# A prompt attention stage with other leads, another order of its first loads, and its weighted sums with the low product first on 64 stationary columns

## The reference, cut to what matters

```python
def stick_breaking_block(q, k, v, q_pos, k_pos):
    z = jnp.einsum('bqhd,bkhd->bhqk', q, k).astype(jnp.float32) * (SB_HEAD_DIM ** -0.5)
    causal = k_pos[None, :] < q_pos[:, None]
    log_beta = jax.nn.log_sigmoid(z)
    log_rem = jnp.where(causal, log_beta - z, 0.0)
    tail = lax.cumsum(log_rem, axis=3, reverse=True) - log_rem
    w = jnp.where(causal, jnp.exp(log_beta + tail), 0.0)
    return jnp.einsum('bhqk,bkhd->bqhd', w.astype(v.dtype), v)

def mla_block(q_nope, q_rope, k_nope, k_rope, v, q_pos, k_pos):
    s = (jnp.einsum('bqhn,bkhn->bhqk', q_nope, k_nope)
         + jnp.einsum('bqhr,bkr->bhqk', q_rope, k_rope)).astype(jnp.float32)
    s = s * ((MLA_NOPE_DIM + MLA_ROPE_DIM) ** -0.5)
    visible = (k_pos[None, :] // CHUNK) <= (q_pos[:, None] // CHUNK)
    s = jnp.where(visible, s, jnp.finfo(jnp.float32).min)
    p = jax.nn.softmax(s, axis=-1)
    return jnp.einsum('bhqk,bkhv->bqhv', p.astype(v.dtype), v)
```

## Time and profile before

| | us |
|---|---|
| median of 3 runs | 2643.04 |
| lowest and highest | 2634.92, 2646.65 |
| the profiled execution, its own time | 2648.48 |
| span of its instructions | 2646.7 |
| prompt attention, first score matmul to last mix | 1089.1 to 2083.7 |
| a head in that stage (first transpose to the next head's first) | 122.9 |

### The profile page before, as it was taken

The page is one execution under the profiler, slowest core; times in us unless marked ns, Lnnn a source line. Parts: engine busy times, 40 slices in busy tenths (PEclk is TensorE's granted clock), DMA queues, the critical chain, the costliest instruction groups (busy, mean ns, idle before and its releaser), DMA issues. The chain is left out here.

```text
span 2646.7 us, 40141 instructions
## 1 busy us (share of the span) xinstructions
PE 2248.5 (85%) x12099; PEld 1869.0 (71%) x12099; DVE 1381.5 (52%) x2759; ACT 1323.5 (50%) x2852; POOL 776.9 (29%) x773
## 2 busy tenths in 40 slices
PE   6599996999977899498989999999989577775887
PEld 1488885899967677286868677777778356664765
DVE  2223232210137333487878778787878388863332
ACT  1223222211112433388888888888888555542221
POOL 0000000000000000356474737465563345542321
PEclk9799998899989899699999999999999777777989
DMA  8333322222337898733323343332320444426773
GB/s 292 106 101 95 108 83 89 100 80 82 116 92 198 284 310 290 158 67 69 68 66 75 70 91 67 68 82 58 74 54 23 107 136 135 142 67 196 177 185 93
DMA packets 304695, 314.44 MB, mean 119 GB/s; under 512 B 88322, under 2 KB 234765, under 8 KB 299489
## 3 DMA queue, kind: packets, MB, share of 16 engines
q1 hardware_dynamic: 299810, 297.45, 40.9%
q10 hardware_dynamic: 3744, 12.19, 1.2%
q0 software_dynamic: 992, 3.21, 0.3%
HBM read 194.83 MB, written 109.57 MB: 115 GB/s over the span
## 5 line engine op out<-in xcount | busy, mean ns | idle before, releaser
L1243 ACT ACTIVATE pa_whi<-banks 128x512 fp32r<-128x512 f32 (+3 forms) x640 | 346.4, 542 | 98.9 <-PE banks L1468 77.9
L1468 PE MATMUL banks<-ident,pa_p 128*128 128x128 f32 x2176 | 354.9, 279 | 2.2 <-ACT pa_p L1208 2.2
L1451 PE MATMUL banks<-pa_khi,pa_qst 128*128 128x512 f32 (+3 forms) x640 | 262.7, 410 | 103.9 <-DVE pa_p L1307 77.1
L1397 POOL TENSOR_TENSOR pa_wlo<-pa_whole,pa_whi 128x512 fp32r<-128x512 f32 (+2 forms) x240 | 279.2, 1172 | 191.4 <-ACT pa_whole L1248 190.7
L1379 POOL CAST pa_khi<-pa_kraw 128x512 fp32r<-128x512 f32 x64 | 39.1, 611 | 993.4 <-DMA pa_kraw<-scratch_sb_kT 993.4
L1468 PEld LDWEIGHTS banks<-ident,pa_p 128*128 128x128 f32 x2176 | 268.5, 143 | 61.4 <-issue 5.6
L1428 PE MATMUL banks<-pa_whi,pa_vst 128*128 128x512 f32 (+3 forms) x640 | 285.1, 445 | 1.5 <-POOL pa_wlo L1397 1.4
L1307 DVE TENSOR_TENSOR_SCAN pa_p<-banks,pa_p,pa_zero 128x512 f32<-128x512 f32 x192 | 246.3, 1283 | 71.4 <-ACT banks L1201 62.6
L1451 PEld LDWEIGHTS banks<-pa_khi,pa_qst 128*128 128x128 f32 x640 | 125.7, 196 | 184.2 <-DVE pa_p L1307 142.7
L1284 DVE TENSOR_TENSOR pa_wlo<-banks,pa_whi 128x512 fp32r<-128x512 f32 (+3 forms) x400 | 234.7, 587 | 27.0 <-ACT pa_whi L1243 27.0
L1452 PE MATMUL banks<-pa_klo,pa_qst 128*128 128x512 f32 (+3 forms) x640 | 242.6, 379 | 0.0
(11 more groups left out here) (231 smaller groups left out, 5095.6 us busy)
## 6 DMA issues: line engine op xcount, KB each, us to landing
ada<-in_ada_w_dram SPq DMA_DIRECT2D x6, 2048.0 KB, 11.4
scratch_sb_kT<-ke_kT SPq DMA_DIRECT2D x12, 1024.0 KB, 8.9
scratch_mla_kT<-ke_nT SPq DMA_DIRECT2D x12, 1024.0 KB, 5.5
scratch_mla_v<-ke_v SPq DMA_DIRECT2D x12, 1024.0 KB, 5.4
co_hlo<-scratch_hT SPq DMA_DIRECT2D x6, 1408.0 KB, 6.9
scratch_gatesT<-co_gates SPq DMA_DIRECT2D x12, 704.0 KB, 10.7
pr_x<-in_x_prompt_dram SPq DMA_DIRECT2D x16, 512.0 KB, 4.4
scratch_hT<-pr_hT SPq DMA_DIRECT2D x16, 512.0 KB, 5.3
```

The costliest lines, as they stand in the source:

```text
L1243: act.activation(whi[:, t % NW, q0:], bank, ACT.Copy).then_inc(hi_done, 1)
L1397: pool.tensor_tensor(wlo[:, t % NW, q0:], whole[:, t % 4, q0:], raw(whi[:, t % NW, q0:]), ALU.subtract).then_inc(pool_lo, 1)
L1451: pe.matmul(bank, qst[job][:, q], khi[job][:, keys], start=True, stop=False)
L1468: y = pe.transpose(ps[:, NS + t % NTB, x * P:(x + 1) * P], probs[g][x][:, i * P:(i + 1) * P], s["ident"][:])
```

## The change

Four edits, all in this stage.

- **Leads.** `LEAD` becomes two numbers: stick chunks run 18 ahead of the steps, softmax chunks 20. `chunks_at` says which chunks a step carries: steps 0 to 19 carry chunk t + 18; steps 20 and 21 carry two each (38 and 39; 40 and 41); steps 22 to 59 carry t + 20; steps 60 and 61 none; steps 62 to 79 carry chunk t - 62 of the next head. The last exponentials stay in steps 60 and 61. Head 0 starts with 18 chunks.
- **First loads.** k and q of the stick half come first, then the mask, `own_tile` and the rotary key, then v.
- **Waits.** TensorE waits at the first chunk of each group for the part of k that the group needs, and for the constants at the first softmax chunk only.
- **The products of a block.** `mix` takes the low product first and then the high one, except in the first block of a softmax group. The low product has only the high part of v as its stationary operand, 64 columns in place of 128, and writes 64 partitions of the bank. The product of the two low parts, which had been added in, is left out.

```diff
@@ constants
-    LEAD = 20
+    STICK_LEAD, SOFT_LEAD = 18, 20
...
@@ which chunks a step carries
-        def chunk_at(h, t, last):
-
-            if t + LEAD < HEAD:
-                return h, t + LEAD
-            return (None, 0) if last else (h + 1, t + LEAD - HEAD)
+        def chunks_at(h, t, last):
+
+            grown = JOB - SOFT_LEAD
+            if t < grown:
+                yield h, t + STICK_LEAD
+            elif t < grown + 2:
+                yield h, 2 * t - grown + STICK_LEAD
+                yield h, 2 * t - grown + STICK_LEAD + 1
+            elif t + SOFT_LEAD < HEAD:
+                yield h, t + SOFT_LEAD
+            if t + STICK_LEAD >= HEAD and not last:
+                yield h + 1, t + STICK_LEAD - HEAD
...
@@ SyncE, first loads
-                for job in range(2):
-                    load_k(0, job)
-                    load_q(0, job)
-                    load_v(0, job)
+                load_k(0, 0)
+                load_q(0, 0)
+                sp.dma_start(causal[:], d["const_causal"]).then_inc(const_loaded, 16)
+                sp.dma_start(probs[3][2][:, 0:CH], d["const_own_tile"]).then_inc(kr_loaded, 16)
+                for i in range(3):
+                    sp.dma_start(early[i * ROPE:(i + 1) * ROPE, 0:T], d["mla_krT"][:, 0:T]).then_inc(kr_loaded, 16)
+                load_v(0, 0)
+                load_k(0, 1)
+                load_q(0, 1)
+                load_v(0, 1)
...
@@ ScalarE, a step
-                    if last and t + LEAD in (HEAD, HEAD + 1):
-                        for g, i, c in exps_at(t + LEAD):
-                            exp(h, g, i, c)
-                    chunk(*chunk_at(h, t, last))
-
-                for m in range(LEAD):
+                    for which in chunks_at(h, t, last):
+                        chunk(*which)
+                    for g, i, c in exps_at(t + SOFT_LEAD):
+                        exp(h, g, i, c)
+
+                for m in range(STICK_LEAD):
...
@@ TensorE, mix
-                    for k, w in enumerate((whi, wlo)):
-                        mm = pe.matmul(ps[:, 6 + n % 2, q0:], vst[job][:, j, :], w[:, t % NW, q0:],
-                                       start=(job == 1 and j == 0 and k == 0), stop=(j == 4 * g + 3 and k == 1))
+
+                    first, done = job == 1 and j == 0, j == 4 * g + 3
+                    high = (ps[:, 6 + n % 2, q0:], vst[job][:, j, :], whi[:, t % NW, q0:])
+                    low = (ps[0:HD, 6 + n % 2, q0:], vst[job][:, j, 0:HD], wlo[:, t % NW, q0:])
+                    if first:
+                        pe.matmul(*high, start=True, stop=False)
+                        mm = pe.matmul(*low, start=False, stop=done)
+                    else:
+                        pe.matmul(*low, start=False, stop=False)
+                        mm = pe.matmul(*high, start=False, stop=done)
                     mm.then_inc(mixed, 1)
...
@@ TensorE, a chunk
+                    if (i, c) == (0, 0):
+
+                        wait_apart(pe, kv_split, kv_upto(h, "k", job) - PARTS + g + 1, passed)
                     if m % JOB == 0:
-                        wait_apart(pe, kv_split, kv_upto(h, "k", job), passed)
                         pe.wait_ge(q_loaded[job], (80 if job else 32) * (h + 1))
+                        if job:
+                            pe.wait_ge(const_done, 1)
```

More of the change, by code:

```diff
@@ L1036, in on_pool @@
         def on_pool(t):
-            return (t + LEAD) % HEAD < JOB and t % 4 != 3
+            return (t + SOFT_LEAD) % HEAD < JOB and t % 4 != 3
         POOLS = sum(on_pool(t) for t in range(HEAD))
@@ L1097, in _ @@
             def _(sp):
-                sp.dma_start(causal[:], d["const_causal"]).then_inc(const_loaded, 16)
-                for i in range(3):
-                    sp.dma_start(early[i * ROPE:(i + 1) * ROPE, 0:T], d["mla_krT"][:, 0:T]).then_inc(kr_loaded, 16)
-                sp.dma_start(probs[3][2][:, 0:CH], d["const_own_tile"]).then_inc(kr_loaded, 16)
                 def load_k(h, job):
@@ L1219, in chunk @@
                 def chunk(h, m):
-                    if h is None:
-                        return
-                    if m < 2 and not (isinstance(h, int) and h == 0):
-                        for g, i, c in exps_at(HEAD + m):
-                            exp(h - 1, g, i, c)
-                        if m == 0:
-                            return
-                        sigmoid(h, 0)
                     if m < JOB:
                         sigmoid(h, m)
-                    for g, i, c in exps_at(m):
-                        exp(h, g, i, c)
                 def finish(h, n):
@@ L1412, in _ @@
                 pe.sem_inc(mixed, NW)
-                pe.wait_ge(const_done, 1)
                 def mix(h, t):
```

2 lines of the change are left out of this document (removed).

## The result

The changed kernel takes 2653.47 us (median of 7 runs, 2650.74 to 2664.82), the kernel before 2644.38 (7 runs beside them, 2634.92 to 2647.82). The ratio over all runs is 1.0047, 95% interval 1.003 to 1.0065: slower by 9 us between the medians, where 17 us less were forecast. The time lies outside the range given, on the other side of no change.

The account below looks back on a forecast made before the run. TensorE was taken to bound softmax chunks (steps 20 to 59), three nearly equal engines the stick chunks. Terms -14.4 - 4 + 0 + 0 + 1.1 = -17.3 us gave 2631.2 from 2648.5, as a median 2626; range 2608 to 2646.

Parts of the forecast that it names:

- The low product on 64 columns: In mix behind the transposes: a shorter weight load saves 0.05 us a step, 14.4 us in softmax steps, 4 in stick.
- The comparison with the keys stage: Keys stage products with 64 stationary columns start 0.27 us apart, against 0.31 in mix; taken as evidence for 0.05 us saved.
- rival 2: In mix, the shorter weight load saves nothing, hidden or otherwise; the total becomes +1.1, 2644 us; chance 0.12.
- The leads: Across each head: 3.0 us gained at the boundary, 3.0 lost at steps 20 and 21; booked 0.
- Steps 20 and 21: Two chunks each: TensorE waits 0.75, 0.4 and 0.9 us; step 22 comes 5.8 us after step 20, 3.0 us lost.
- The boundary to step 68: Between heads, one wait of 4.55 us becomes two of 2.0 and 1.6; step 68 starts 2.6 us earlier.
- The 32 pairs from step 68 to 20: Step-and-chunk pairs after the boundary: as before, except two smaller chunks, about 0.4 us less.
- The loads: At the stage's start, the first scan waits for the rotary key and comes 1.1 us later.
- Rival 1: At the head boundary: waits at steps 20 and 21 shrink, up to 21 us more saved, about 2605 to 2612; chance 0.15.
- Rival 3: At steps 20 and 21 the clock drops and the boundary yields only 1.1 us: +9.6, 2653 us; chance 0.13.

Follow-up runs that it names:

- e1_products: Kernel before with only the products changed (low product first, on 64 columns): 2644.6 us, ratio 1.0013.
- e4_turned: Kernel before with the low product on 64 columns but behind the high one, except in a group's last block: 2648.4 us, ratio 1.0019.
- e5_both64: Kernel before with both products on 64 columns, high one first, some blocks excepted, part of the output left out: 2643.25 us in one run.
- e11_mix_last64: Kernel before with the output products moved behind the step's score products, low one first and on 64 columns: 2665.53 us, ratio 1.0074.
- e2_leads: Kernel before with the two leads alone (18 for stick chunks, 20 for softmax chunks): 2657.9 us, ratio 1.0063.
- e3_loads: Kernel before with the new order of first loads and the finer TensorE waits alone: 2645.96 us, ratio 1.0017.
- e6_half: Kernel before with three of a block's four transposes cut to 64 rows, part of the values left out: 2735.94 us in one run.
- e8_turn22: Kernel before with only the back edge of the loop over heads moved from step 12 to step 22: 2665.75 us, ratio 1.0064.

## Why the prediction was wrong

**The low product on 64 columns: forecast -14.4 and -4, measured 0. This step failed.** It read 0.07 to 0.08 us of a distance of 0.31 as waiting for weights. e1_products shows no gain, e4_turned and e5_both64 none with the load in question at 64 columns. What stands in the 0.31 us is worked out from the rows: the printed start of a matmul behind the transposes is no measure of when it begins to stream. Before, the weight loads behind the transposes of the earlier trace rows stand so:

```profile
1571.11 0.19 PEld L1428 LDWEIGHTS banks<-pa_whi,pa_vst 128*128 128x128 f32 x1
1571.22 0.19 PEld L1428 LDWEIGHTS banks<-pa_wlo,pa_vst 128*128 128x128 f32 x1
1571.46 0.19 PEld L1451 LDWEIGHTS banks<-pa_khi,pa_qst 128*128 128x128 f32 x1
```

In these rows a load runs one matmul ahead. The one at 1571.22 can start when the last transpose is through, and 0.24 us later, at 1571.46, the next one does, since the first product is through: 512 columns take no less anywhere in these rows. That leaves no wait for weights, and its printed start, 1571.14, is by my estimate about 0.08 us too early. After, the loads stand at 1570.98 and 1571.09, 0.11 apart although the first is 0.05 shorter. The comparison with the keys stage failed on what stands ahead, which the prediction called equally short: there it is matmuls of 64 columns, shorter than a load, as behind the mask's product in e11_mix_last64 (0.26); here it is transposes of 128 columns, whose starts are 0.11 us apart like those of the loads. This is rival 2, given 0.12. By the rule of the Trainium skill ("TensorE: Matmul & The Clock Gate", on the phases of a matmul), the next weights load under the present matmul; the trace agrees at the very place where I set it aside, and the mask's product (0.32 us with the wide load, 0.26 with the narrow one) shows its limit.

**The leads: forecast 0, measured +10.9 over six heads of the change and +6.8 in e2_leads, which has them alone (in the change with +4.2 in the last head, which has only the loss, and -2.2 in head 0). This step failed too.** The products and the loads add -0.7 and +1.0 by themselves. The other 4 us I put down to the clock (not tried apart): within the six heads it is at half for 44.4 us in the change and 34.1 in e2_leads. Before has 41.0, so the clock explains little of the change's loss and none of that of e2_leads. The parts of the 10.9:
- *Steps 20 and 21*: forecast 3.0 lost, measured 3.0 to 3.1. Right, wait by wait (0.66, 0.24 and 0.75 us for 0.75, 0.4 and 0.9).
- *The boundary to step 68*: forecast 2.6 gained, with one stretch of half clock. From step 60 to 68 it is 15.97 us before; after, 13.52 in heads with 3.4 us at half clock (2.45 gained) and 14.0 to 14.6 in heads with 6.8 (1.4 to 2.0 gained). In e2_leads a head with none takes 12.74. The walk was right for its clock. That the clock stays down for 6.8 us in most heads is no proof against the two short waits, though: e3_loads, which has the one wait of 4.55 us, has 6.8 us at all six boundaries, e5_both64 at five, e1_products at none. One of those of e3_loads:

```profile
1574.39:1581.21 6.82, 4.45 (x14) 3.67 (x15) 2.83 (x4) 4.38 (x12) 2.74 (x4) 0.50 0.91 204
```

- *The 32 pairs from step 68 to 20*: forecast 0.4 gained "as before". This failed. Before, and then two heads after:

```profile
1588.38:1638.06 49.68, 45.30 (x242) 33.86 (x241) 39.76 (x45) 42.65 (x92) 40.26 (x40) 0.97 0.18 41
```

```profile
1713.51:1764.41 50.90, 44.89 (x242) 33.81 (x241) 39.23 (x45) 42.73 (x93) 40.69 (x40) 0.97 0.19 44
1589.89:1639.66 49.77, 43.62 (x243) 32.65 (x241) 38.97 (x44) 42.53 (x93) 40.30 (x40) 1.00 0.18 42
```

At the same granted clock (0.97) it is 1.2 us longer; without a fall of the clock it is as long as before with one. Most of it shows in steps 0 to 11, before and after:

```profile
1605.98:1623.00 17.02, 15.61 (x88) 11.66 (x86) 14.44 (x18) 15.24 (x35) 12.45 (x13) 1.00 0.27 62
```

```profile
1607.25:1625.31 18.06, 15.69 (x87) 11.65 (x86) 15.57 (x18) 15.29 (x35) 12.92 (x15) 1.00 0.28 64
```

TensorE and ScalarE do the same work, VectorE has 1.13 us more between these two steps, and the stretch is 1.04 longer: other scans now fall beside these steps. That the order of VectorE's scans and low parts decides is my reading; which pairs of step and chunk do it was not tried apart.

So a boundary gains 1.3 us on average (the 65.6 us of steps 60 to 79 and 0 to 19 become 64.0 to 64.9), not 3.0, and the 3.0 are lost in full: 1.7 a head, 6 x 1.7 = 10.2 of the 10.9. Seen whole, what counts is when the 40 scans of the next head are through, since the softmax chunks wait for their banks. The prediction carried TensorE's gain at step 68 on to step 20 and did not ask whether the scans had gained it too. Before, the first one starts 7.09 us after step 60 (1572.41):

```profile
1579.50 1.00 DVE L1307 TENSOR_TENSOR_SCAN pa_p<-banks,pa_causal 128x128 f32<-128x128 f32 x2 [5.24 <-ACT banks L1201]
```

and the last one ends at 1640.30, 67.9 us after step 60 (68.5 in one head). After, the first starts 0.54 us later, from first to last they take 61.8 to 62.6 us where they took 60.8 (61.4 in one head), and the last ends 69.4 to 70.2 us after step 60 (at 1645.00 here); heads 2 to 6. The 2.6 us by which step 68 is ahead never reach the scans.

**The loads: forecast +1.1, measured +1.3.** Right, by a figure that varies by some 0.5 us either way between kernels with the same loads.

**The rivals.** Rival 1 (the boundary closes) fell: steps 20 and 21 take 5.9 us, not under 4. Rival 3's figure, 2653, is the time measured, but that is luck: of its two parts the fall of the clock at steps 20 and 21 is not there (it stays at 1.00 in steps 20 to 22), and its sum keeps the 18.4 us of the products. Its other part, a boundary that yields 1.1 us in place of 3.0, is close to the 1.3 measured. The clock falls at steps 64 and 15, as it fell at 63 and 14 before. The sum of what was right and what failed, 0 + 10.9 - 2.2 + 4.2 + 1.3, is 14.2 from the first memset, against 9.1 between the medians and 12.9 within the stage from its first scan. The range was too narrow for the prediction's own bounds: with 0 for the products, a loss of 1.9 at each of seven boundaries and loads 2 us later the sum is +15.3, 2658. Each failure had its rival; both at once were given no chance of their own.

## What to carry to other kernels

Before pricing a shorter weight load, look at what runs ahead of it: it pays only where that matmul is shorter than the load, and the distance between two weight loads shows this better than that between two matmul starts, of which the first may be early. When a wait is moved to another place of a loop, walk the whole loop at the granted clock of each stretch: the chain that made the wait (here 40 scans) may start later and take longer, as it did here, while the steps beside it look faster. To judge a change within one stage, measure several repetitions of its loop inside the trace; six heads of the five kernels with the old leads, the old edge and the old place of the products (before, e1_products, e3_loads, e4_turned, e5_both64) lie within 2.1 us (736.5 to 738.6), while the total of the kernel before goes from 2628 to 2657 over 31 runs.

## What the hardware showed beside

- **Rows of the stationary operand.** Going from 128 to 64 rows and back costs some 0.2 us a step: 133.1 us a head for 122.9, with a load that starts 0.29 us after the last is done (e6_half; its transposes also stream 64 columns in place of 128).
- **The back edge of a hardware loop** at step 22 stops ScalarE for 3.59 and VectorE for 5.85 us, both put down to issue (e8_turn22). Its place matters: 3.2 us a head in the stick half, 5.5 to 7.6 in the softmax half.
- **The granted clock** fell to 0.50 behind the boundary's two waits in some heads and not in others of the same execution (e2_leads: 6.8, 0 and 6.8 us in heads 2 to 4), so a head takes 122.6 to 125.5 us in one run. With one wait of 4.55 us it varies as well: 3.4 us at five of six boundaries before, 6.8 at all six in e3_loads.
